# Order of the routing stage around the last output projection in a FoX and differential attention layer with a mixture of experts

## The chip, the cores and the metric

The kernel runs on one core of one Trainium2 chip. The metric is the device time of one execution in microseconds (us). Engines are named as in the profile: PE is the matmul engine, PEld its weight load, DVE the vector engine, ACT the scalar engine, POOL the GpSimd engine, and SP the queue that issues the DMA transfers.

## The reference, cut to what matters

One layer handles 256 prompt rows and 8 x 16 sample rows of width 1024, 384 rows in all (three row tiles of 128). Attention ends in an output projection with a residual. Then comes the mixture of experts, which the change is about:

```python
h = h + o @ w_out                                   # (384, 1024)
hn = h * rsqrt(mean(h * h) + 1e-6) * ffn_norm
logits = hn @ w_router + b_router                   # 32 experts
top_val, top_idx = top_k(logits, 4); gates = softmax(top_val)
# for each expert e, over the rows that chose it:
hcat = hn[rows] @ w_gate_up[e] + b_gate_up[e]       # (., 2048)
glu, lin = min(hcat[:, 0::2], 7), clip(hcat[:, 1::2], -7, 7)
y[rows] += gate * ((glu * sigmoid(1.702 * glu) * (lin + 1)) @ w_down[e] + b_down[e])
```

All data is float32. The weights of the 32 experts are 32 x (8 MB + 4 MB) and are streamed from HBM once.

## The kernel before, in words

Every engine has its own program, in an order written out by hand; they meet at semaphores (`wait_ge` and `then_inc`). There is no planner. `link` makes an engine wait for its own last instruction.

**The projection.** `project_out(n)` is one column half of one row tile (tile n // 2, half n % 2): 8 products of 128x128 by 128x512, each recorded as two passes, so 16 rows of the trace (L1672). DVE adds each half to the residual rows y in `residual(n)` (L1233, semaphore y_added).

**Routing a row tile t.** PE turns the tile (`turn_rows`, 8 transposes, L1706), ACT and DVE move four turned blocks each to SBUF with the norm's gain (`hT_evac`, L897 and L1250), PE forms the 32 logits (`logits`, L1715, 16 passes). ACT sums the squares (`square`, L879), DVE makes the mean, ACT the root (`root`, L884), DVE the reciprocal (`invert`, L1256), ACT scales the rows to x2n (`scale`, L889). DVE's `route` (L1265 to L1273) finds the four best experts and the 0/1 table M of rows by experts, `gate` the softmax weights. PE's order is: halves 2, turn 0, half 3, logits 0, half 4, turn 1, half 5, logits 1, turn 2, logits 2.

**Ranks, selection, gather.** After that PE multiplies M by a strictly triangular table `before` and by ones (L1734 to L1740), which gives each row's rank within its expert. DVE forms the table RK from it (L1313 to L1317). POOL's `build_sel` compares two columns of RK (the two experts of a pair) with 0..63 and so makes a selection matrix `sel` of 384 x 128 slots (L662, six instructions), then one with the gates in it, `selg` (L672). `gather` on PE multiplies x2n by `sel` (24 products, 48 passes, L1750); ACT and DVE move the result to XT (L927, L1339).

**The pairs.** Sixteen pairs of experts follow (`run_pairs`). In each, PE adds the bias (L1759), runs the gate and up products (128 passes of 512 columns, L1769), gathers for the next pair, and runs the down products (64 passes, L1801) and the scatter (L1816). The weights come in 2 MB pieces, 12 for a pair and 192 in all, through a ring of 8 slots. The first 8 pieces are loaded ahead (the last two of them after half 5, since the slots hold the projection's weights until then); each of the other 184 is issued by SP (L533) when PE has freed a slot (piece_done). PE frees the first two slots after the first quarter of the first pair's gate and up products.

Of the kernel before, what the change touches and what calls it, by code (L numbers as in the profile page):

```python
# [89 lines left out]
def build(nc, io, out):  # L90
    ctx = ExitStack()
    with ctx:
# [105 lines left out]
        rt = at(a0 + 11264, 512)  # L198
        bgu4 = at(hn0, 512)
# [4 lines left out]
        pRK = [at3(hn0 + 2336 + 16 * i, 3, 2) for i in range(2)]  # L204
        pG = [at3(hn0 + 2336 + 16 * i + 8, 3, 2) for i in range(2)]
        pO = at(hn0 + 2368, 1)
        OVI = at(hn0 + 2370, 164).bitcast(I32)
        IDX = at(hn0 + 2536, 8).bitcast(U32)
        own_e = [at(hn0 + 2544 + 128 * i, P) for i in range(2)]
        before = at(hn0 + 2800, P)  # L210
# [47 lines left out]
        rank_done, table_done = sem("rank_done"), sem("table_done")  # L258
# [77 lines left out]
        copy_no = {j: n + 1 for n, j in enumerate(copies)}  # L336

# [63 lines left out]
        def _(sp):  # L401
# [97 lines left out]
            for b in range(2, BATCH_D + 2):  # L499
                if b < BATCH_D:  # L500
                    sp.wait_ge(kc_T, 4 * (b - 1))
                    load_cache(b, "k")
                if b >= 4:
                    sp.wait_ge(mixed, NP + 2 * (b - 4) + 2)
                    load_cache(b - 2, "v")
                    load_v3(b - 2)
                if b in (4, 5):
                    s = {4: 5, 5: 3}[b]
                    sp.dma_start(piece_slot(s), piece_src(0, s - LEAD)).then_inc(ring_in[s], 16)
            sp.wait_ge(scored, NA)  # L510
# [8 lines left out]
            sp.dma_start(before, io["before"][:, :]).then_inc(s_bef, 16)  # L519
# [48 lines left out]
        def _(g_):  # L568
# [77 lines left out]
            def build_sel(u, pair, at_, r=None):  # L646
# [12 lines left out]
                for t in range(3):  # L659
                    for x in range(2):  # L660
                        cols = slice(SLOTS * x, SLOTS * (x + 1))
                        last = nc.gpsimd.tensor_scalar(sel[u][:, t, cols], C["iota"], pRK[u][:, t, x:x + 1], None, ALU.is_equal)  # L662
                last.then_inc(sel_ready, 1)

                nc.gpsimd.tensor_copy(own_e[u].rearrange("p (x s) -> p x s", x=2),
                                      C["eye4"][:, bass.ds(pair * 2, 2)].unsqueeze(2).to_broadcast([P, 2, SLOTS]))
                g_.wait_ge(gates_ready, 1)
                lk(nc.gpsimd.tensor_copy(pG[u], GT[:, :, bass.ds(pair * 2, 2)]))
                for t in range(3):
                    for x in range(2):  # L670
                        cols = slice(SLOTS * x, SLOTS * (x + 1))
                        last = nc.gpsimd.tensor_scalar(selg[u][:, t, cols], C["iota"], pRK[u][:, t, x:x + 1],  # L672
                                                       pG[u][:, t, x:x + 1], ALU.is_equal, ALU.mult)
                last.then_inc(selg_ready, 1)

            g_.wait_ge(table_done, 1)
            for u in range(2):
                build_sel(u, u, lambda c, u=u: 2 * u + c)
# [15 lines left out]
        def _(ac):  # L694
# [182 lines left out]
            def square(t):  # L877
                ac.wait_ge(y_added, 2 * t + 2)
                link(nc.scalar.activation(junk2, y[:, t], ACT.Square, accum_out=stat[:, 20 + t:21 + t]))  # L879
                nc.scalar.activation(stat[:, 40:41], stat[:, 20:21], ACT.Copy).then_inc(h_sq, 1)  # L880
# [11 lines left out]
            def hT_evac(t):  # L892
                ac.wait_ge(h_T, t + 1)
                if t == 2:
                    ac.wait_ge(logit_done, 1)
                for k in range(4):
                    last = nc.scalar.activation(XTr[t][:, k], banks[0][:, P * k:P * (k + 1)], ACT.Copy,  # L897
                                                scale=gcol[:, 8 + k:9 + k])
# [8 lines left out]
            root(0)  # L907
# [37 lines left out]
            gathered(lambda k, c: c, 0)  # L945
            run_pairs(ac, lambda it, u, at_, nx: pair(at_, u, nx))
# [11 lines left out]
        def _(ve):  # L958
# [281 lines left out]
            def mean(t):  # L1240
                ve.wait_ge(h_sq, t + 1)
                nc.vector.tensor_scalar(stat[:, 20 + t:21 + t], stat[:, 20 + t:21 + t], 1.0 / D, EPS, ALU.mult, ALU.add
                                        ).then_inc(h_ms, 1)

            def hT_evac(t):
                ve.wait_ge(h_T, t + 1)
                if t == 2:
                    ve.wait_ge(logit_done, 1)
                for k in range(4):
                    last = nc.vector.tensor_scalar(XTr[t][:, 4 + k], banks[1][:, P * k:P * (k + 1)],  # L1250
                                                   gcol[:, 12 + k:13 + k], None, ALU.mult)
                last.then_inc(hT_v, 1)

            def invert(t):
                ve.wait_ge(h_rt, t + 1)
                nc.vector.reciprocal(stat[:, 24 + t:25 + t], stat[:, 24 + t:25 + t]).then_inc(h_rc, 1)  # L1256
                ve.wait_ge(h_rc, t + 1)

            def route(t):
# [3 lines left out]
                ix = rt[:, 16 * t + 8:16 * t + 16]  # L1263
                ve.wait_ge(logit_done, t + 1)
                link(nc.vector.scalar_tensor_tensor(out=L, in0=banks[(2, 6, 7)[t]][:, 0:32], scalar=stat[:, 24 + t:25 + t],  # L1265
# [5 lines left out]
                link(nc.vector.tensor_scalar(M[:, t], C["iota"][:, 0:E], ix[:, 0:1], None, ALU.is_equal))  # L1271
                for j in range(1, TOPK):
                    ins = nc.vector.scalar_tensor_tensor(out=M[:, t], in0=C["iota"][:, 0:E], scalar=ix[:, j:j + 1],  # L1273
                                                         in1=M[:, t], op0=ALU.is_equal, op1=ALU.add)
                    if j < TOPK - 1:
                        link(ins)
                ins.then_inc(route_done, 1)

            def gate(t):

                ix = rt[:, 16 * t + 8:16 * t + 16]
                g4 = rt[:, 64 + 16 * t:68 + 16 * t]
                tmp = [rt[:, 256 + 32 * j:288 + 32 * j] for j in range(3)]
# [3 lines left out]
                nc.vector.tensor_scalar(GT[:, t], C["iota"][:, 0:E], ix[:, 0:1], g4[:, 0:1], ALU.is_equal, ALU.mult)  # L1287
                for j in range(1, TOPK):
                    ins = nc.vector.tensor_scalar(tmp[j - 1], C["iota"][:, 0:E], ix[:, j:j + 1], g4[:, j:j + 1],
                                                  ALU.is_equal, ALU.mult)  # L1290
                link(ins)
                for j in range(1, TOPK):
                    link(nc.vector.tensor_tensor(GT[:, t], GT[:, t], tmp[j - 1], ALU.add))

            residual(2)
            mean(0)
            hT_evac(0)
            residual(3)
            invert(0)
            mean(1)  # L1300
            route(0)
            gate(0)
            residual(4)
            hT_evac(1)
            invert(1)
# [6 lines left out]
            ve.wait_ge(rank_done, 1)  # L1312
            nc.vector.scalar_tensor_tensor(out=RK[:, 0], in0=banks[2][:, 0:E], scalar=1.0, in1=M[:, 0],  # L1313
                                           op0=ALU.add, op1=ALU.mult)
# [85 lines left out]
        def _(pe):  # L1400
# [354 lines left out]
            def pair(at_, u, arrived, next_at=None):  # L1755
# [6 lines left out]
                for k in range(8):  # L1762
                    if k % 2 == 0:
                        s = [arrived(k + x) for x in range(2)]
# [109 lines left out]
```

## Time and profile before

| | us |
|---|---|
| median of three runs | 1288.69 |
| lowest and highest run | 1286.04, 1290.76 |
| the profiled execution, whole | 1290.47 |
| its span from first to last instruction | 1288.7 |

In the profiled execution the matmul engine is busy for 95% of the span, DVE for 28%, ACT for 15% and POOL for 12%. The mean granted clock of the matmul engine is 0.972 of full speed. The core reads 442 MB from HBM. The page cuts the span into 40 slices of some 32 us; the routing stage lies in the slices from 300 to 354 us, and everything after it is the sixteen pairs. A busy share of a whole span hides such stages, so the rows further down are of single stretches.

### The profile page before, as it was taken

Reading aid. Unit: us, or ns where it says so; the run is one execution under the profiler, and the core shown is the slowest. Engines: PE = TensorE matmul, PEld = TensorE weight load, DVE = VectorE, ACT = ScalarE, POOL = GpSimd, SP = SyncE. Lnnn points to the kernel's source line nnn. Section 1 sums busy time; section 2 is a strip of 40 time slices with the busy share of each in tenths; the row PEclk is TensorE's granted clock in tenths of the full one; section 3 lists DMA queues with packets and bytes.
Section 4 is the critical chain, followed back from the end, with each engine's and each line's share of the span. In section 5 each row is a group of like instructions: output and inputs, shape, how many; then the busy total and the mean of one; then the engine's idle time right before and its main releaser. Section 6 shows DMA issues by size and latency. Waiting matters only on the chain.

```text
span 1288.7 us, 16163 instructions
## 1 busy us (share of the span) xinstructions
PE 1229.9 (95%) x6079; PEld 545.4 (42%) x6080; DVE 354.7 (28%) x947; ACT 198.4 (15%) x523; POOL 158.3 (12%) x378
## 2 busy tenths in 40 slices
PE   7999989899899999999999999999999999999987
PEld 3444355554643434344343434343443434343422
DVE  2233355532422212142221212131321212131412
ACT  3211264322400101010010101010100101010100
POOL 0032302110302021020202022020202020120000
PEclk9999997989799999999999999999999999999998
DMA  8712521961379999999999999999999999999993
GB/s 266 272 53 105 213 82 66 356 215 83 145 324 427 427 429 428 428 430 427 429 429 426 430 429 427 430 429 427 429 430 427 429 429 427 429 429 427 427 429 146
DMA packets 55049, 447.53 MB, mean 347 GB/s; under 512 B 11089, under 2 KB 11490, under 8 KB 30434
## 3 DMA queue, kind: packets, MB, share of 16 engines
q1 hardware_dynamic: 54400, 446.87, 83.6%
q8 instruction: 24, 0.39, 0.1%
q10 hardware_dynamic: 610, 0.14, 0.0%
q14 instruction: 15, 0.12, 0.0%
HBM read 442.13 MB, written 4.86 MB: 347 GB/s over the span
## 4 chain that ended last, share of the span: by engine, by line
PE 67%; DMA 27%; DVE 3%; ACT 1%; issue 1%; POOL 1%; SPq 1%; ACTq 0%; POOLq 0%; DVEq 0%
DMA arena<-in_w_gate_up 24%; PE psum L1801 17%; PE psum L1769 17%; PE psum L1506 8%; PE psum L1750 7%; PE psum L1672 3%; PE psum L1816 2%; PE psum L1784 1%; PE psum L1780 1%; DMA arena<-in_w_in 1%; PE psum L1543 1%; DMA arena<-in_cache_diff_k 1%; PE psum L1640 1%; PE psum L1573 1%; PE psum L1561 1%
## 5 line engine op out<-in xcount | busy, mean ns | idle before, releaser
L1769 PE MATMUL psum<-arena 128*64 128x512 f32 x2048 | 450.6, 599 | 20.7 <-DMA arena<-in_w_gate_up 20.2
L1769 PEld LDWEIGHTS psum<-arena 128*64 128x64 f32 x2048 | 153.2, 138 | 316.2 <-issue 316.2
L1801 PE MATMUL psum<-arena 128*64 128x512 f32 x1024 | 224.6, 596 | 0.8
L1366 DVE TENSOR_SCALAR arena<-psum 128x256 f32<-128x256 f32 x64 | 26.7, 417 | 434.1 <-PE psum L1769 432.3
L1801 PEld LDWEIGHTS psum<-arena 128*64 128x64 f32 x1024 | 78.7, 138 | 135.9 <-issue 134.6
L1506 PE MATMUL psum<-arena 128*128 128x512 f32 x288 | 128.7, 601 | 5.0 <-DMA arena<-in_w_in 4.5
L934 ACT ACTIVATE arena<-arena 128x256 f32<-128x256 f32 x64 | 26.7, 417 | 632.6 <-DVE arena L1366 632.6
L1750 PEld LDWEIGHTS psum<-arena 128*128 128x128 f32 x768 | 89.8, 197 | 16.1 <-issue 16.1
L1750 PE MATMUL psum<-arena 128*128 128x128 f32 x768 | 92.8, 282 | 3.9 <-POOL arena L662 3.9
L655 POOL COPY arena<-arena 128x6 f32 (+1 forms) x16 | 3.0, 190 | 759.4 <-PE psum L1801 704.3
L1816 PE MATMUL psum<-arena 128*128 128x512 f32 x192 | 93.2, 622 | 0.0
L1506 PEld LDWEIGHTS psum<-arena 128*128 128x128 f32 x288 | 53.9, 192 | 70.3 <-issue 63.3
L1384 DVE TENSOR_TENSOR arena<-psum,arena 128x512 f32<-128x512 f32 x96 | 66.4, 692 | 25.3 <-PE psum L1816 25.3
L1379 DVE COPY arena<-psum 128x512 f32<-128x512 f32 x16 | 11.1, 692 | 219.6 <-PE psum L1801 219.6
L1816 PEld LDWEIGHTS psum<-arena 128*128 128x128 f32 x192 | 28.6, 188 | 64.3 <-DVE arena L1384 42.1
L672 POOL TENSOR_SCALAR arena<-arena 128x64 f32<-128x64 f32 x96 | 54.1, 586 | 0.0
L1672 PE MATMUL psum<-arena 128*128 128x512 f32 x96 | 42.4, 595 | 1.0 <-DVE arena L1233 1.0
L662 POOL TENSOR_SCALAR arena<-arena 128x64 f32<-128x64 f32 x96 | 40.4, 448 | 0.0
L1354 DVE TENSOR_TENSOR arena<-arena 128x256 f32<-128x256 f32 x64 | 36.4, 610 | 5.4
L942 ACT ACTIVATE arena<-psum 128x512 f32<-128x512 f32 x16 | 9.6, 599 | 162.0 <-PE psum L1801 162.0
L1368 DVE SCALAR_TENSOR_TENSOR arena<-arena 128x256 f32<-128x256 f32 x64 | 27.3, 426 | 2.2
L1672 PEld LDWEIGHTS psum<-arena 128*128 128x128 f32 x96 | 17.8, 190 | 22.1 <-issue 20.6
(239 smaller groups left out, 810.6 us busy)
## 6 DMA issues: line engine op xcount, KB each, us to landing
arena<-in_w_gate_up SPq DMA_DIRECT2D x128, 2048.0 KB, 25.1
arena<-in_w_down SPq DMA_DIRECT2D x64, 2048.0 KB, 23.0
arena<-in_w_in SPq DMA_DIRECT2D x5, 2048.0 KB, 14.6
arena<-in_cache_fox_k SPq DMA_DIRECT2D x8, 512.0 KB, 5.6
arena<-in_cache_diff_k SPq DMA_DIRECT2D x8, 512.0 KB, 6.4
arena<-in_cache_fox_v SPq DMA_DIRECT2D x8, 512.0 KB, 6.8
arena<-in_cache_diff_v SPq DMA_DIRECT2D x8, 512.0 KB, 8.1
arena<-in_w_out SPq DMA_DIRECT2D x4, 1024.0 KB, 7.1
```

The costliest lines, as they stand in the source:

```text
L662: last = nc.gpsimd.tensor_scalar(sel[u][:, t, cols], C["iota"], pRK[u][:, t, x:x + 1], None, ALU.is_equal)
L672: last = nc.gpsimd.tensor_scalar(selg[u][:, t, cols], C["iota"], pRK[u][:, t, x:x + 1], pG[u][:, t, x:x + 1], ALU.is_equal, ALU.mult)
L934: nc.scalar.activation(sg[n % 2], tg[n % 2], ACT.Sigmoid, scale=1.702).then_inc(sig_ready, 1)
L1354: nc.vector.tensor_tensor(act_rows[:, 32 * n:32 * (n + 1)], ta[n % 2].rearrange("s (p q) -> s p q", q=8), sg[n % 2].rearrange("s (p q) -> ...
L1368: lk(nc.vector.scalar_tensor_tensor(out=ta[n % 2], in0=tl[n % 2], scalar=1.0, in1=tg[n % 2], op0=ALU.add, op1=ALU.mult))
L1384: nc.vector.tensor_tensor(y[:, t, cols], banks[4 + n % 2], y[:, t, cols], ALU.add).then_inc(y_added, 1)
L1506: last = mm(z_bank(u), hnT[:, k, r0:r0 + n], wv[:, k], start=(k == 0), stop=(k == 7))
L1672: last = mm(banks[4 + n % 2], oT[:, k, P * t:P * (t + 1)], wv[:, k % 2, 512 * hf:512 * hf + 512], start=(k == 0), stop=(k == 7))
L1750: last = mm(banks[6 + k // 4][:, P * (k % 4):P * (k % 4 + 1)], x2n[:, t, P * k:P * (k + 1)], sel[u][:, t], start=(t == 0), stop=(t == 2))
L1769: last = mm(banks[n][half], XT[u][:, k, half], piece_slot(s[x])[:, c0:c0 + 512], start=False, stop=(k == 7), skip_group_check=True)
L1801: last = mm(banks[hf][half], actT[:, 4 * i + c, half], w, start=False, stop=(i == 1 and c == 3), skip_group_check=True)
L1816: mm(banks[4 + n % 2], gT[:, P * t:P * (t + 1)], rows[:, 512 * hf:512 * hf + 512], start=True, stop=True).then_inc(scat_done, 1)
```

## The change

- The last row tile is handled by column halves: `turn_rows`, `hT_evac`, `logits` and the squares take a part of the blocks each, so that the left half is done before the right half of the projection is. A turned block k now lies where `turned_row(k)` says.
- PE's order: the turn of tile 1 stands in the middle of half 4; half 5 holds the left turn of tile 2 (before its product 4) and the ranks of tiles 0 and 1 (before its product 6). Then the left logits, the right turn, the gather's products of tiles 0 and 1 with the right logits between them, the last tile's ranks, its gather, and the totals.
- DVE's table is made in two steps; POOL builds the selection of tiles 0 and 1 in `first_two`, DVE that of tile 2. The table keeps rank plus 1 and is compared with `places` = 1..64.
- `route` and `gate` compare all four choices in one instruction of 128 elements and add them up in one reduction (EQ, EG), in place of chains of 32-element instructions.
- POOL computes the norm's inverse root as a power of -0.5 (`inverse`), in place of DVE's mean, ACT's root and DVE's reciprocal.
- `gates(2)` and `gate(2)` come after the first gather has been moved to XT. In a pair PE waits for `own_ready` at the bias, for the ACT half of XT at product 0, for the DVE half at product 4, and for `selg` only at its turning.
- `before` is loaded ahead of the residual rows, not after half 5.

```diff
-            def root(t):
-                ac.wait_ge(h_ms, t + 1)
-                nc.scalar.activation(stat[:, 24 + t:25 + t], stat[:, 20 + t:21 + t], ACT.Sqrt).then_inc(h_rt, 1)
+            def inverse(t):
+                ms = stat[:, 20 + t:21 + t]
+                g_.wait_ge(h_sq, t + 1 + (t == 2))
+                if t == 2:
+                    nc.gpsimd.tensor_tensor(ms, ms, stat[:, 46:47], ALU.add).then_inc(h_ms, 1)
+                    g_.wait_ge(h_ms, 3)
+                nc.gpsimd.tensor_scalar(ms, ms, 1.0 / D, EPS, ALU.mult, ALU.add).then_inc(h_ms, 1)
+                g_.wait_ge(h_ms, t + 1 + (t == 2))
+                nc.gpsimd.tensor_tensor(stat[:, 24 + t:25 + t], ms, stat[:, 44:45], ALU.pow).then_inc(h_rc, 1)
+            def first_two():
+                pr = pRK[0][:, 0:2]
+                g_.wait_ge(first_table, 1)
+                nc.gpsimd.tensor_copy(pr, RK[:, 0:2, 0:2]).then_inc(p_first, 1)
+                g_.wait_ge(p_first, 1)
+                for t in range(2):
+                    for x in range(2):
+                        last = nc.gpsimd.tensor_scalar(sel[0][:, t, SLOTS * x:SLOTS * (x + 1)], places,
+                                                       pr[:, t, x:x + 1], None, ALU.is_equal)
+                last.then_inc(sel_ready, 1)
@@ POOL
+            inverse(0)
+            inverse(1)
+            g_.wait_ge(places_ready, 1)
+            first_two()
+            g_.wait_ge(bias_kept, 4)
+            own_rows(0, 0)
+            inverse(2)
             g_.wait_ge(table_done, 1)
@@ ACT
             square(0)
-            root(0)
             hT_evac(0)
             scale(0)
             square(1)
-            root(1)
+            hT_evac(1)
             gates(0)
-            hT_evac(1)
             scale(1)
-            square(2)
-            hT_evac(2)
-            root(2)
+            square_half(0)
+            hT_evac(2, (0, 1))
+            gates(1)
+            square_half(1)
+            hT_evac(2, (4, 5))
             scale(2)
-            gates(1)
-            gates(2)
@@ DVE, route
-                link(nc.vector.tensor_scalar(M[:, t], C["iota"][:, 0:E], ix[:, 0:1], None, ALU.is_equal))
-                for j in range(1, TOPK):
-                    ins = nc.vector.scalar_tensor_tensor(out=M[:, t], in0=C["iota"][:, 0:E], scalar=ix[:, j:j + 1],
-                                                         in1=M[:, t], op0=ALU.is_equal, op1=ALU.add)
+                link(nc.vector.tensor_tensor(EQ[t], C["iota"][:, 0:E].unsqueeze(2).to_broadcast([P, E, TOPK]),
+                                             ix[:, 0:TOPK].unsqueeze(1).to_broadcast([P, E, TOPK]), ALU.is_equal))
+                nc.vector.tensor_reduce(M[:, t], EQ[t], AX.X, ALU.add).then_inc(route_done, 1)
@@ DVE, order
+            route(1)
+            hT_evac(2, (2, 3))
+            gate(1)
+            ve.wait_ge(rank_done, 1)
+            table(0, banks[2][:, 4 * E:5 * E])
+            table(1, banks[2][:, 5 * E:6 * E]).then_inc(first_table, 1)
             residual(5)
-            hT_evac(2)
-            mean(2)
-            route(1)
-            invert(2)
+            hT_evac(2, (6, 7))
             route(2)
+            ve.wait_ge(rank_done, 2)
+            table(2, banks[2][:, 6 * E:7 * E]).then_inc(table_done, 1)
+            ve.wait_ge(table_done, 1)
+            ve.wait_ge(places_ready, 1)
+            for x in range(2):
+                last = nc.vector.tensor_scalar(sel[0][:, 2, SLOTS * x:SLOTS * (x + 1)], places, RK[:, 2, x:x + 1], None,
+                                               ALU.is_equal)
+            last.then_inc(last_sel, 1)
@@ PE, order
-            project_out(4)
-            turn_rows(1)
-            project_out(5)
+            project_out(4, {4: lambda: turn_rows(1)})
             logits(1)
-            turn_rows(2)
-            logits(2)
+            project_out(5, {4: lambda: turn_rows(2, (0, 1, 2, 3)), 6: ranks_of_two})
+            logits(2, (0, 1, 2, 3))
+            turn_rows(2, (4, 5, 6, 7))
+            gather_first(0, (0, 1, 2, 3))
+            logits(2, (4, 5, 6, 7))
+            gather_first(0, (4, 5, 6, 7))
+            gather_first(1, range(8))
+            ranks_of_last()
+            gather_first(2, range(8))
+            totals()
```

## Rows read from the trace of the kernel before

**Rows 1.** Busy time by stretch: PE, PEld, DVE, ACT, POOL, granted clock, DMA share, GB/s.

```profile
410.10:466.40 56.30, 56.30 (x281) 22.62 (x277) 13.31 (x28) 5.67 (x12) 6.79 (x17) 1.00 1.01 426
629.00:688.00 59.00, 56.93 (x277) 23.16 (x277) 13.71 (x29) 5.68 (x12) 7.02 (x18) 1.00 1.00 427
```

**Rows 2.** The chain that ended last, in the pairs: start, length, what.

```profile
353.61 27.69 PE psum L1769 x128
381.29 5.55 PE psum L1750 x48
...
409.06 1.07 PE psum L1759 x8
410.13 27.62 PE psum L1769 x128
...
629.67 28.79 DMA arena<-in_w_gate_up
...
688.27 28.96 DMA arena<-in_w_gate_up
```

**Rows 3.** SP's own timeline, 330 to 420 us: start, length, what was issued.

```profile
330.75 1.82 SPq L521 DMA_DIRECT2D arena<-in_b_gate_up  x4
332.61 0.89 SPq L523 DMA_DIRECT2D arena<-in_b_down  x2
333.54 0.90 SPq L525 DMA_DIRECT2D arena<-in_w_gate_up  x2
360.86 7.75 SPq L533 DMA_DIRECT2D arena<-in_w_down  x4
```

**Rows 4.** The chain that ended last, 315 to 354 us.

```profile
315.65 6.95 PE psum L1672 x16
...
330.34 1.71 PE psum L1715 x16
332.05 0.92 PE psum L1706 x8
...
352.12 1.14 DVE arena L1339 x4
```

**Rows 5.** Timeline of DVE in the routing of tile 1: start, length, instruction.

```profile
334.10 0.24 DVE L1265 SCALAR_TENSOR_TENSOR arena<-psum,arena 128x32 f32<-128x32 f32 x1
...
335.17 0.24 DVE L1271 TENSOR_SCALAR arena<-arena 128x32 f32<-128x32 f32 x1
335.44 0.83 DVE L1273 SCALAR_TENSOR_TENSOR arena<-arena 128x32 f32<-128x32 f32 x3
```

**Rows 6.** Groups by line and shape, whole span: busy, mean ns, idle before.

```profile
L662 POOL TENSOR_SCALAR arena<-arena 128x64 f32<-128x64 f32 x96 | 40.4, 448 | 0.0
L635 POOL TENSOR_TENSOR arena<-arena 128x1 f32<-128x1 f32 x16 | 8.9, 556 | 1.3
...
L1354 DVE TENSOR_TENSOR arena<-arena 128x256 f32<-128x256 f32 x64 | 36.4, 610 | 5.4
...
L1069 DVE TENSOR_REDUCE arena<-arena 128x8 f32<-128x512 f32 x12 | 8.2, 686 | 49.1 <-ACT arena L781 49.1
...
L1233 DVE TENSOR_TENSOR arena<-psum,arena 128x512 f32<-128x512 f32 x6 | 4.0, 688 | 18.5 <-PE psum L1672 18.5
...
L1293 DVE TENSOR_TENSOR arena<-arena 128x32 f32<-128x32 f32 x9 | 1.7, 192 | 0.3
```

**Rows 7.** Stretches of 1 us, PE alone: length, busy, clock, DMA share, GB/s.

```profile
335.00:336.00 1.00, 1.00 (x11) 0.96 0.29 115
...
349.00:350.00 1.00, 1.00 (x8) 0.71 0.00 0
```

**Rows 8.** Timeline of PE where it resumed after waits: idle before in brackets.

```profile
299.07 7.13 PE L1672 MATMUL psum<-arena 128*128 128x512 f32 x16 [0.97 <-DVE arena L1233]
...
334.22 2.04 PE L1715 MATMUL psum<-arena 128*128 128x32 f32 x16 [1.26 <-ACT arena L897]
...
343.53 8.48 PE L1750 MATMUL psum<-arena 128*128 128x128 f32 x48 [3.85 <-POOL arena L662]
```

More of the change, by code:

```diff
@@ L658, in build_sel @@
                     lk(nc.gpsimd.tensor_scalar(pRK[u], pRK[u], pO, None, ALU.subtract))
[L659 to L666, printed above, removed]
+                if not first:
+                    for t in range(3):
+                        for x in range(2):
+                            cols = slice(SLOTS * x, SLOTS * (x + 1))
+                            last = nc.gpsimd.tensor_scalar(sel[u][:, t, cols], places, pRK[u][:, t, x:x + 1], None,
+                                                           ALU.is_equal)
+                    last.then_inc(sel_ready, 1)
+                    own_rows(u, pair)
                 g_.wait_ge(gates_ready, 1)
@@ L1237, in _, with hT_evac @@
             residual(1)
[L1240 to L1246, printed above, removed]
+            def hT_evac(t, ks=(2, 3, 6, 7)):
+                ve.wait_ge(h_T, t + 1 + (ks[0] == 6))
                 if t == 2:
                     ve.wait_ge(logit_done, 1)
-                for k in range(4):
-                    last = nc.vector.tensor_scalar(XTr[t][:, 4 + k], banks[1][:, P * k:P * (k + 1)],
-                                                   gcol[:, 12 + k:13 + k], None, ALU.mult)
+                for k in ks:
+                    last = nc.vector.tensor_scalar(XTr[t][:, k], turned_row(k), gcol[:, 8 + k:9 + k], None, ALU.mult)
                 last.then_inc(hT_v, 1)
[L1254 to L1257, printed above, removed]
             def route(t):
@@ L1286, in gate @@
                 link(nc.vector.tensor_scalar(g4, g4, stat[:, 32 + t:33 + t], None, ALU.mult))
[L1287 to L1293, printed above, removed]
+                link(nc.vector.tensor_tensor(EG, EQ[t], g4.unsqueeze(1).to_broadcast([P, E, TOPK]), ALU.mult))
@@ L1295, in _, with table @@
+                link(nc.vector.tensor_reduce(GT[:, t], EG, AX.X, ALU.add))
+            def table(t, rank):
+                return nc.vector.scalar_tensor_tensor(out=RK[:, t], in0=rank, scalar=1.0, in1=M[:, t],
+                                                      op0=ALU.add, op1=ALU.mult)
             residual(2)
-            mean(0)
             hT_evac(0)
             residual(3)
-            invert(0)
-            mean(1)
             route(0)
+            hT_evac(1)
             gate(0)
@@ L1713, in logits @@
                 pe.wait_ge(s_wrt, 16)
-                for k in range(8):
-                    last = mm(banks[(2, 6, 7)[t]][:, 0:32], XTr[t][:, k], w_rt[:, k], start=(k == 0), stop=(k == 7))
-                last.then_inc(logit_done, 1)
+                for k in ks:
+                    last = mm(banks[(2, 6, 3)[t]][:, 0:32], XTr[t][:, k], w_rt[:, k], start=(k == 0), stop=(k == 7))
+                if k == 7:
+                    last.then_inc(logit_done, 1)
+            R = banks[2][:, 4 * E:7 * E]
@@ new lines, in totals, with gather_first @@
+            def totals():
+                for t in range(3):
+                    last = mm(banks[4][:, 0:E], C["ones"], M[:, t], start=(t == 0), stop=(t == 2))
+                last.then_inc(rank_done, 1)
+            def gather_first(t, ks):
+                pe.wait_ge(h_n, t + 1)
+                pe.wait_ge(last_sel if t == 2 else sel_ready, 1)
+                for k in ks:
+                    last = mm(banks[6 + k // 4][:, P * (k % 4):P * (k % 4 + 1)], x2n[:, t, P * k:P * (k + 1)], sel[0][:, t],
+                              start=(t == 0 and k % 4 == 0), stop=(t == 2), skip_group_check=True)
+                    if t == 2 and k % 4 == 3:
+                        last.then_inc(xg_done, 1)
```

127 lines of the change are left out of this document (67 added, 60 removed).

## The prediction

> **What bounds the kernel now.** I read the profile in four steps: the pairs first, since they are three quarters of the time, then what sets their start, then the stage that the change touches, then the clock.
>
> The stretches of the pairs [rows 1] show PE and DMA both near 100%, which doesn't say which of them leads. The chain of waits does [rows 2]. An early pair takes 410.13 - 353.61 = 56.52 us, all of it PE work. From 629.67 on the chain goes through a transfer of gate and up weights in every pair, and a pair takes 688.27 - 629.67 = 58.60 us. So PE's need is 56.5 and DMA's is 58.6 us for a pair. DMA is the slower one; PE only lives on the ring's stock for the first pairs, and DMA is already at 1.01 of its time in the second pair, at 426 GB/s [rows 1]. The end is therefore set by the first refill plus 184 pieces of 58.60 / 12 = 4.88 us, and a tail on PE behind the last piece that the change doesn't touch.
>
> When is the first refill? SP issued the last two preloaded pieces at 333.54 and the first refill at 360.86 [rows 3]; at 335 to 336 us DMA was busy only in part, and at 349 us it was at zero [rows 7]. It is idle until PE frees two slots, 360.86 - 353.61 = 7.25 us after the first pair's first product. What moves the start of the first pair at 353.61 thus moves the end by as much, one to one, as long as the two preloaded pieces aren't what limits DMA.
>
> The start of the pair in turn hangs on the stage from 315.65 (half 4 begins) to 353.61, which is 37.96 us. In it the chain runs over PE alone up to 332.05 + 0.92 [rows 4], and then over DVE, PE and POOL by turns: PE stood for 1.26 us before the last logits and for 3.85 us before the gather [rows 8], and the gather took 8.48 us against 5.55 us for the same 48 passes in the pair [rows 2, 8]. The granted clock explains that: it fell from 1.0 to 0.5 (2.4 to 1.2 GHz) at the end of the stretch at 335 us, after the wait of 1.26 us, and rose again during 349 us [rows 7].
>
> **The change part by part, as what PE still has to do from 315.65 to the first product.** All at full clock.
> - Halves 4 and 5: 2 x 6.95 = 13.90 [rows 4].
> - Turns of tiles 1 and 2, 16 transposes at 0.92 for 8: 1.84. Logits 1 and 2: 2 x 1.71 = 3.42 [rows 4]. Splitting them adds no passes.
> - Ranks: 3 + 2 products and 3 for the totals, 16 passes. Before, six products with the same task ran mostly at half clock; the nearest row at full clock is the logits with 16 passes of 32 columns, 1.71 [rows 4]. One of the eight has 64 columns. I take 1.71.
> - The gather, same 48 passes in another order: 5.55. Bias: 1.07 [rows 2].
> Sum 27.49 us. Now the waits, by walking through the engines.
>
> Half 4 with its turn ends at 315.65 + 6.95 + 0.92 = 323.5; logits 1 follow at once, since the turned blocks of tile 1 are moved (1.14 us, as the four instructions in [rows 4]) while half 4's last products run. They end at 325.2. Half 5 with half a turn (0.46) and 6 rank passes (0.64) ends at 325.2 + 6.95 + 1.10 = 333.3. That is 3.0 us later than before (330.34), and it is what residual 5, the bias loads and pieces 6 and 7 wait for.
>
> Is the work inside half 5 ready? A route takes 335.17 - 334.10 = 1.07 us up to L1271 and then 0.24 + 0.83 and links, 2.2 in all [rows 5]. The four 32-element instructions become a comparison and a sum of 128 elements. The trace has neither: a tensor operation costs 0.19 us at 32 elements and 0.61 at 256, a reduction 0.69 at 512 [rows 6]. Interpolated by size I take 0.3 for each, so 1.7 for a route; the bounds are 0.2 and 0.65 each, 1.5 to 2.4. Route 1 starts with logits 1 at 325.2 and ends at 326.9, before PE comes to the ranks at some 330.9. Behind it on DVE stand two moves (to 329.9) and gate 1 (about 1.1, its chain of seven 32-element instructions gone; to 331.5). DVE then waits for the ranks, with residual 5 queued behind that wait. Ranks end at 331.5, two tables of 0.2 end at 332.0, and residual 5 is wanted only at 333.3: no cost, 1.3 us to spare. POOL's copy and four comparisons of 0.45 [rows 6] give the selection at 332.0 + 0.3 + 1.8 = 334.1.
>
> PE after half 5: left logits 333.3 to 334.15; residual 5 (0.69 [rows 6]) ends at 334.0; right turn to 334.65; gather of tile 0, left, to 335.6, its selection just ready; right logits need two moves of 0.3 on each of DVE and ACT, ready 335.5: to 336.45. Then 12 products of gather, 2.8 us, to 339.2. Meanwhile route 2 runs from 336.45 to 338.2. It also needs the inverse root: squares of the right half (ACT, 334.0 to 334.9), an addition, a mean and a power of 0.56 [rows 6] on POOL, so 336.0. That is 0.45 us before it is wanted, and what ACT's root, the reciprocal and their table loads cost is off the path anyway, as it was before behind route 1. Scaling of tile 2 (2.1 us) is done at 338.1, before its gather.
>
> The last tile's ranks take 0.45 after 339.2. Then comes the one bare wait: table 0.25, two comparisons on DVE about 0.45 (the trace has 0.24 for 32 elements [rows 5]; 0.4 to 0.7), handovers 0.15, together 0.85. The last gather's eight products follow. ACT's and DVE's moves to XT (1.14, on the path before [rows 4]) now lie beside totals and bias (0.65 + 1.07) and product 4's wait: nothing, and if that cover were gone 1.14. `gates(2)`, `gate(2)` and the second table of gates have until the pair's end. I add 0.3 for the small handovers between the pieces.
>
> So 27.49 + 0.85 + 0.30 = 28.64 us in place of 37.96: **9.3 us** less. The first product comes at 344.3, the first refill at 351.5. Pieces 6 and 7 are issued 3.0 us later less nothing but the 0.33 us of `before`, so at 336.2; together they are 2 x 4.88 us and end near 347. DMA still stands idle from there to 351.5, so the preload doesn't limit. Loading `before` ahead of y puts 64 KB, far less than 1 us, into a stretch where half 0 doesn't need y yet. In the loop itself `places` for the iota and a third semaphore change no instruction's size, and PE's later waits can win nothing where DMA leads.
>
> The granted clock is what I am least sure of. The Trainium skill ("TensorE: Matmul & The Clock Gate", section "A second HAM failure mode: psum-queue depth-cycling") says that frequent short idles between groups of matmuls make the clock swing between half and full rate. That speaks against the new order, which changes the kind of work ten times in 11 us; the trace agrees as far as the fall at 335 us goes, and the sum above stands at full clock, while with the rule it would be the first rival's.
>
> There is one rule on ports too. The Trainium skill ("SBUF — State Buffer", section "SBUF: two separate sides") states that DVE with two SBUF inputs and GpSimd reading SBUF shut each other out. POOL's selection here runs beside gate 1's end at most; by the rule it would cost one comparison of 0.3 us, a sum of 9.0 in place of 9.3.
>
> **The rivals.**
> - **The clock falls in the new order too.** For it: 1.26 us of waiting and thin work brought it down before [rows 7, 8]. Against: 0.97 us of waiting before half 2 didn't, since that half then ran 16 passes in 7.13 us [rows 8], and my longest wait is 0.85. Price: the same gather lost 8.48 - 5.55 = 2.9 us at half clock. If it falls before the last gather it also takes in totals, bias and the start of the pair: at most twice that, 6. Then the gain is 6.4, at worst 3.4: 1282.3, at worst 1285.3.
> - **The handovers cost more.** The walk has PE meeting its inputs within 0.1 us at three places (selection, right logits, inverse root). If DVE's 128-element instructions are at their upper bound, gate 1 is 0.7 later and the selection with it; each of three places may cost 0.5 to 1. Gain 7.3: 1281.4.
> - **It doesn't matter.** If DMA weren't the limit, or the preload was, the gain would be swallowed. [Rows 1, 2] speak against it: there is no idle DMA in any pair after the refills begin. Result 1288.7.
> - **Slower: half clock from within half 5 on.** The turn and ranks inside half 5 break its dense run. If DVE's route 1 came late there, PE would stand in the middle of the projection and the clock would drop at 331. PE work from there to the first product is some 13 us at full clock, and the first quarter of the pair, 7.25, lies behind it: all at half clock would cost 20 us against 9.3 gained, so 1299. It decides from about 9.3 us of PE work at half clock on. Before, half clock lasted 13 us of which PE worked 9, so that far it doesn't reach; and route 1 has 4 us to spare.
>
> **How the numbers follow.** Full clock as summed: 0.50. Clock falls: 0.25. Handovers: 0.17. No effect: 0.05. Slower: 0.03. The profiled execution took 1290.47 us, 1.8 above its span and 1.8 above the median of 1288.69; the sum gives 1281.2 for it and for the median 1288.69 - 9.3 = **1279.4**. The three runs spread by 2.4 us to either side, and 0.3% (3.9 us) is what can be told from no change. Low end: DVE's new instructions at their lower bound and no extra handovers give 0.8 more, and 1.6 for the spread: 1277.0. High end: the clock's worst price, 1285.3. Faster by over 0.3% means below 1284.8: all of the first three cases but the clock's worst part, 0.88. Within 0.3%: 0.09. Slower: 0.03.
>
> **What would show it.** Right: the first L1769 of the changed kernel at 344 to 345, the first refill some 7 us after it, half 5's last pass near 333, a single PE wait of about 0.85 before the last gather, and a DMA-led chain from about pair 4 or 5 on with 58.6 us for a pair. If the clock fell, a stretch of 0.5 stands between 336 and 352. Wrong: a PE wait of over 1 us at the selection of tiles 0 and 1 or inside half 5; DMA with gaps after the first refill; or pairs longer than 58.6 us, which nothing here foretells.

## The result, and the profile after

The changed kernel takes 1275.17 us (median of 10 executions, 1272.21 to 1282.28), the kernel before 1288.63 us (median of 10, 1283.35 to 1295.47). The medians lie 13.5 us apart. The ratio of the two over all their executions is 0.9903, with a 95% interval from 0.9877 to 0.9929: faster by 12.5 us, between 9.1 and 15.9. The forecast was 1279.4, its range 1277.0 to 1285.3. The time lies below the range. The gain of 9.3 us that was summed lies just inside the measured interval, so the first question is whether the sum or the range was at fault.

The profiled execution took 1273.09 us, with a span of 1271.3. This is its chain of work that ended last, from half 4 to the seventh pair (start, length, what), the answer to [rows 2, 4]:

```profile
310.04 3.52 PE psum L1700 x8
313.55 0.87 PE psum L1734 x8
314.43 3.44 PE psum L1700 x8
317.86 1.70 PE psum L1742 x16
319.57 3.52 PE psum L1700 x8
...
327.63 0.81 PE psum L1742 x8
329.07 0.89 PE psum L1770 x8
329.96 0.91 PE psum L1742 x8
330.87 2.76 PE psum L1770 x24
334.83 2.02 PE psum L1770 x16
337.45 1.07 PE psum L1810 x8
338.52 27.62 PE psum L1821 x128
...
614.43 28.77 DMA arena<-in_w_gate_up
...
673.01 28.92 DMA arena<-in_w_gate_up
```

Between half 4 and the first gate and up product (L1821 here, L1769 before) the chain has only two pieces that aren't PE's, the table and the selection of tile 2 on DVE (L1317 and L1341, 0.20 and 0.44 us), and none of POOL. Half 4 begins at 310.04, the first product at 338.45 in the timeline: the stage takes 28.41 us, where before it took 353.61 - 315.65 = 37.96 [rows 2, 4]. The sum had said 28.64. In the pairs nothing has changed: 673.01 - 614.43 = 58.58 us for one, through DMA.

The timeline of the last tile (all engines, start, length, idle before in brackets):

```profile
331.86 0.17 DVE L1301 CAST arena<-arena 128x8 f32<-128x8 uint32 x1
332.07 0.29 DVE L1302 TENSOR_TENSOR arena<-arena 128x128 f32<-128x128 f32 x1
332.39 0.29 DVE L1304 TENSOR_REDUCE arena<-arena 128x32 f32<-128x128 f32 x1
...
334.03 0.19 DVE L1317 SCALAR_TENSOR_TENSOR arena<-psum,arena 128x32 f32<-128x32 f32 x1 [1.35 <-PE psum L1759]
334.26 0.43 DVE L1341 TENSOR_SCALAR arena<-arena 128x64 f32<-128x64 f32 x2
...
334.83 2.02 PE L1770 MATMUL psum<-arena 128*128 128x128 f32 x16 [0.84 <-DVE arena L1341]
```

The two new DVE instructions take 0.29 us each (estimate 0.3), and the one bare wait is 0.84 us (estimate 0.85). SP and the clock stretches answer to [rows 3, 7]:

```profile
330.35 0.90 SPq L533 DMA_DIRECT2D arena<-in_w_gate_up  x2
345.73 7.75 SPq L541 DMA_DIRECT2D arena<-in_w_down  x4
```

```profile
334.00:335.00 1.00, 0.17 (x1) 1.00 1.04 442
...
342.00:343.00 1.00, 1.00 (x8) 1.00 0.00 0
```

The granted clock stays at 1.00 through the wait, and DMA stands idle from 342 us to the first refill at 345.73: the preload didn't become the limit. The sharing of ports between DVE and POOL that the prediction weighed didn't arise at the selection of tiles 0 and 1: gate 1 ended at 325.58, before POOL's copy at 326.36, and POOL's four comparisons took 1.71 us (estimate 1.8).

So the stage gave 9.55 us in this pair of traces, but the profiled executions differ by 1290.47 - 1273.09 = 17.4 us. The rest lies outside the stage: half 4 begins 315.65 - 310.04 = 5.6 us earlier, and from the first refill to the end of the span it is 1271.3 - 345.73 = 925.6 us in place of 1288.7 - 360.86 = 927.8. The projection ahead of half 4, where the change does alter some instructions of the other engines, is not the place. Here is its first half, before and then after:

```profile
283.88 7.13 PE L1672 MATMUL psum<-arena 128*128 128x512 f32 x16
```

```profile
278.26 7.13 PE L1700 MATMUL psum<-arena 128*128 128x512 f32 x16
```

From there to half 4 it is 31.8 us in both (315.65 - 283.88 and 310.04 - 278.26), and so in the further traces of either kernel in experiments 1, 2, 9 and 10. The 5.6 us thus lie ahead of the projection. Two theories were tested:
- **Chance:** the clock in the attention and behind the last transfer differs from execution to execution, and the change gives what the stage gives.
- **Systematic:** the stage before costs more than its one trace shows, or the change shortens something ahead of or behind it.

### The profile page after: what moved, and what is told of

It is laid out like the page before. It is cut to its first block, busy times and chain, and to the rows that moved or that the text cites. A ratio compares the mean times of both kernels' runs of the same rounds, so it can differ in the third digit from the quotient of the medians.

```text
span 1271.3 us, 16137 instructions
## 1 busy us (share of the span) xinstructions
PE 1217.8 (96%) x6083; PEld 536.0 (42%) x6084; DVE 350.7 (28%) x922; ACT 192.1 (15%) x515; POOL 160.4 (13%) x385
## 4 chain that ended last, share of the span: by engine, by line
PE 67%; DMA 27%; DVE 2%; ACT 1%; issue 1%; SPq 1%; POOL 0%; ACTq 0%; POOLq 0%
DMA arena<-in_w_gate_up 25%; PE psum L1854 18%; PE psum L1821 17%; PE psum L1532 9%; PE psum L1801 7%; PE psum L1700 3%; PE psum L1869 2%; PE psum L1836 1%; PE psum L1832 1%; PE psum L1569 1%; DMA arena<-in_cache_diff_k 1%; DMA arena<-in_w_in 1%; PE psum L1599 1%; PE psum L1587 1%; PE psum L1666 1%
## 5 line engine op out<-in xcount | busy, mean ns | idle before, releaser
L1821 PE MATMUL psum<-arena 128*64 128x512 f32 x2048 | 448.8, 597 | 20.4 <-DMA arena<-in_w_gate_up 20.4
L1821 PEld LDWEIGHTS psum<-arena 128*64 128x64 f32 x2048 | 150.9, 138 | 316.4 <-issue 316.3
L1801 PEld LDWEIGHTS psum<-arena 128*128 128x128 f32 x720 | 81.5, 192 | 12.2 <-issue 12.2
L1801 PE MATMUL psum<-arena 128*128 128x128 f32 x720 | 84.4, 276 | 0.0
L1532 PEld LDWEIGHTS psum<-arena 128*128 128x128 f32 x288 | 54.5, 194 | 69.6 <-issue 64.7
L1869 PEld LDWEIGHTS psum<-arena 128*128 128x128 f32 x192 | 28.6, 188 | 64.3 <-DVE arena L1405 42.1
L706 POOL TENSOR_SCALAR arena<-arena 128x64 f32<-128x64 f32 x96 | 54.2, 583 | 0.0
L697 POOL TENSOR_SCALAR arena<-arena 128x64 f32<-128x64 f32 x90 | 37.6, 443 | 0.0
L1110 DVE TENSOR_REDUCE arena<-arena 128x8 f32<-128x512 f32 (+1 forms) x14 | 9.6, 685 | 61.6 <-ACT arena L823 61.6
```

What stands on the lines that cost most here:

```text
L697: last = nc.gpsimd.tensor_scalar(sel[u][:, t, cols], places, pRK[u][:, t, x:x + 1], None, ALU.is_equal)
L706: last = nc.gpsimd.tensor_scalar(selg[u][:, t, cols], places, pRK[u][:, t, x:x + 1], pG[u][:, t, x:x + 1], ALU.is_equal, ALU.mult)
L1532: last = mm(z_bank(u), hnT[:, k, r0:r0 + n], wv[:, k], start=(k == 0), stop=(k == 7))
L1801: last = mm(banks[6 + k // 4][:, P * (k % 4):P * (k % 4 + 1)], x2n[:, t, P * k:P * (k + 1)], sel[u][:, t], start=(t == 0), stop=(t == 2))
L1821: last = mm(banks[n][half], XT[u][:, k, half], piece_slot(s[x])[:, c0:c0 + 512], start=False, stop=(k == 7), skip_group_check=True)
L1869: mm(banks[4 + n % 2], gT[:, P * t:P * (t + 1)], rows[:, 512 * hf:512 * hf + 512], start=True, stop=True).then_inc(scat_done, 1)
```

## The experiments

Each kernel was timed beside the kernel before, with 6 to 12 executions, except for experiment 12 with a single one. "Mean" is over all timed executions of a kernel, leaving out one of 2.5 ms (experiment 4) and one of 4.4 ms (experiment 1). "The stage" runs from the start of half 4 to the first gate and up product. "Half clock time" is the time in which the granted clock was 0.5: 2 x (1 - mean granted clock) x time.

**1, 9: the kernel before, unchanged.**

> The kernel before, unchanged, run against itself. It measures how much of a difference of two kernels is chance, and gives a second trace of the stage. Theory A (the stage gives 9.5 us in every execution, and what the timed difference has beyond that lies in the clock of stretches that the change doesn't touch): ratio 1.000 within its interval, the stage from half 4 to the first gate and up product again about 38 us, and the start of half 4 at another place than 315.65 us, anywhere from 310 to 320. Theory B (the stage before loses more to half clock than the one trace shows, since its clock stretch may last into the first pair): the stage takes 39 us or more, with the same start of half 4.

> The kernel before, unchanged, once more, for its trace and for more executions. Theory chance: the start of half 4 lies between 308 and 320 us as in the traces of the changed kernel, the stage takes 36.8 to 38 us, and over all executions the difference of the two kernels settles between 9 and 10.5 us. Rival (the change also shortens what lies ahead of the stage or behind it, by 2 us or more): the half clock time ahead of half 4 is again over 30 us, where the traces of kernels with the new order have 17 to 44, mean 31, and the difference settles at 12 us or more.

Ratios 1.0002 (0.9978 to 1.0027) and 1.0002 (0.9971 to 1.0033). PE where it resumed before the last gather, and at the first pair, in the first and in the second:

```profile
344.69 7.38 PE L1750 MATMUL psum<-arena 128*128 128x128 f32 x48 [3.84 <-POOL arena L662]
...
353.67 8.80 PE L1769 MATMUL psum<-arena 128*64 128x512 f32 x40 [0.52 <-DVE arena L1339]
```

```profile
339.50 7.06 PE L1750 MATMUL psum<-arena 128*128 128x128 f32 x48 [3.86 <-POOL arena L662]
...
348.15 4.08 PE L1769 MATMUL psum<-arena 128*64 128x512 f32 x18 [0.52 <-DVE arena L1339]
```

Half 4 began at 316.83 and 311.61, so the stage took 36.84 and 36.54 us. The waits are those of [rows 8] to 0.02 us; what differs is the gather, 8.48, 7.38 and 7.06 us, since the half clock lasted shorter. The stage before thus costs 37.1 us on average of three, not more than its first trace showed but less. The part of the systematic theory that has a costlier stage falls.

**2, 10: the changed kernel, unchanged.**

> The changed kernel, unchanged, again. Theory A: the stage from half 4 to the first gate and up product takes 28.5 us, and the start of half 4 moves by some us from run to run with the clock in the attention stage; the timed gain over before comes nearer to 9.5 us than the 13.5 us of the medians first seen. Theory B: the timed gain stays at 12 to 14 us, because before loses more at the stage than its trace showed.

> The changed kernel, unchanged, once more. Theory chance: stage 28.4 us, start of half 4 between 308 and 320 us, mean of the executions near 1278. Rival: mean near 1276.

Ratios 0.9924 (0.9896 to 0.9953) and 0.9916 (0.9884 to 0.9948). The stage took 28.41 us both times, but half 4 began at 315.11 and 310.25. The clock between (stretches of PE: length, busy, clock, DMA share, GB/s), in the first repetition and then in the second:

```profile
160.00:240.00 80.00, 71.97 (x523) 0.81 0.29 102
240.00:300.00 60.00, 53.19 (x530) 1.00 0.81 295
```

```profile
160.00:240.00 80.00, 71.92 (x578) 0.89 0.35 129
240.00:300.00 60.00, 55.31 (x491) 0.97 0.74 267
```

The same program had a mean clock of 0.81 or 0.89 in the same 80 us of attention. The kernel before had 0.87, 0.74 and 0.87 there in its three traces. Over all traces the start of half 4 lies between 308.6 and 317.2 us, for either order of the stage.

**3: before, with its waits filled.**

```diff
             turn_rows(2)
+            filler(5)
             logits(2)
 ...
+            filler(16)
             pe.wait_ge(s_bgu, 64)
+def filler(n): for _ in range(n): mm(banks[4][:, 0:P], C["ones"], C["ones"], start=True, stop=True)
```

> The kernel before with 5 extra products of ones ahead of the last logits and 16 ahead of the first gather, which keep PE busy in its two long waits. Their results are written to a PSUM bank that nobody reads. If the half clock of the stage is what a good part of the gain came from: the clock stays at 1.0, the gather takes 5.6 instead of 8.5 us, and the kernel is 3 to 3.5 us faster than before (0.9975). If the clock falls anyway or the extra products lie in the way: no gain, or 1 us slower.

Mean 1285.5 us against 1287.7; ratio 0.9984 (0.9957 to 1.0012), which timing alone can tell neither from no change nor from the expected 0.9975. Its PE timeline:

```profile
340.14 0.41 PE L1744 MATMUL psum<-arena 128*128 128x32 f32 x2 [1.12 <-DVE arena L1273]
340.61 5.45 PE L1720 MATMUL psum<-arena 128*128 128x128 f32 x32
345.89 5.52 PE L1756 MATMUL psum<-arena 128*128 128x128 f32 x48
...
353.01 9.23 PE L1775 MATMUL psum<-arena 128*64 128x512 f32 x42 [0.52 <-DVE arena L1339]
```

The gather took 5.52 us, as it does in the pairs. But the clock fell once more, from 341 to 345 us, and the fill of 16 products took 5.45 us where the wait was 3.85. The stage took 35.84 us: 1.3 under the mean of before. The expected 3 to 3.5 us didn't come in the stage: the gather gained 2.1 us on the mean of the three traces of before (7.64), but the fill, cut too long for the clock at which it ran, took 1.6 us more than the wait. It shows that the clock's share of the gather is 1.5 to 3 us (7.06 to 8.48, less 5.52).

**4: changed, the gather no longer fills the wait for the last route.**

```diff
-            gather_first(0, (0, 1, 2, 3))
             logits(2, (4, 5, 6, 7))
-            gather_first(0, (4, 5, 6, 7))
-            gather_first(1, range(8))
             ranks_of_last()
+            gather_first(0, range(8))
+            gather_first(1, range(8))
```

> The changed kernel with the gather of tiles 0 and 1 moved behind the last tile's ranks, so that it no longer fills the wait for the last logits and route. Prediction by the walk through the engines: PE now waits some 2.5 us for the last route, while the gather of tiles 0 and 1 hides the table and the selection of tile 2: net 2 us slower than the changed kernel if the clock stays at 1.0, 4 to 5 us slower if the wait of 2.5 us brings it down as it did in the kernel before. A rival (the order doesn't matter since DMA has room): no difference from the changed kernel.

```profile
336.49 1.05 PE L1742 MATMUL psum<-arena 128*128 128x32 f32 x8 [0.75 <-ACT arena L940]
337.38 0.39 PE L1757 MATMUL psum<-arena 128*128 128x32 f32 x2
339.41 0.64 PE L1759 MATMUL psum<-arena 128*128 128x32 f32 x2 [1.64 <-DVE arena L1304]
339.86 7.90 PE L1770 MATMUL psum<-arena 128*128 128x128 f32 x48
```

```profile
337.00:338.00 1.00, 0.77 (x7) 0.92 0.62 158
338.00:339.00 1.00, 0.00 (x0) 0.50 1.17 281
```

Half 4 began at 316.71 and the first product came at 349.34: 32.63 us, 4.2 more than the changed kernel; mean 1281.8, ratio 0.9952 (0.9927 to 0.9976). PE waited 0.75 and 1.64 us, and the 48 passes took 7.90 us in place of 5.55. The clock fell to 0.5 within the stretch at 337 us, whose mean is 0.92, that is as the second wait began and not after it. Of the 4.2 us, 2.35 are the clock's in the gather and the other 1.9 are put down to the order by subtraction. The size expected (4 to 5 us with a fall) held; that it would be the long wait that brings the clock down did not.

**5: changed, first pair later by 40 products.**

```diff
             gather_first(2, range(8))
+            for _ in range(40):
+                mm(banks[5][:, 0:P], C["ones"], C["ones"], start=True, stop=True)
             totals()
```

> The changed kernel with 40 extra products of ones (80 passes, 9.3 us) ahead of the totals, so that the first pair starts later by what the change took from the stage. Their results are written to a PSUM bank that nobody reads. Theory DMA leads from the first refill on: first gate and up product, first refill and the end all move by 9.3 us, 1277.2 (mean of 19 executions of the changed kernel) becomes 1286.5, which is within 2 us of before. Rival (a part of the stage's gain is given back later anyway, by the ring's stock): the end moves by less than 7 us.

```profile
341.76 9.10 PE L1792 MATMUL psum<-arena 128*128 128x128 f32 x80
...
352.45 13.10 PE L1823 MATMUL psum<-arena 128*64 128x512 f32 x60
```

Half 4 began at 315.11 as in experiment 2's trace, the first product came 8.93 us later than there, and the span was 1287.1 against 1278.6: 8.5 us. Mean 1289.1, ratio 0.9995 (0.9976 to 1.0015); the expected 1286.5 was 2.6 lower, and without one execution of 1303.2 us the mean is 1287.8. All of the stage's gain is undone by moving the start of the pairs alone. The rival, an end that moves by less than 7 us, is out.

**6: changed, 7 more products in each pair.**

```diff
                 pe.wait_ge(act_ready, at_(4, 4))
+                for _ in range(7):
+                    mm(banks[4][:, 0:P], C["ones"], C["ones"], start=True, stop=True)
                 for c in range(8):
```

> The changed kernel with 7 extra products of ones (14 passes, 1.6 us) in each of the 16 pairs, ahead of the turning of the activations, written to a PSUM bank before its next use. Theory DMA leads: PE's need per pair rises from 56.4 to 58.0 us and stays under DMA's 58.6, so 15 pairs cost nothing and only the last one's 1.6 us are seen: 1278.8. Rival (PE leads, or both do in turn): 16 x 1.6 = 26 us more, 1303.

The chain of two early pairs, and who PE waited for in all the pairs (total, times, longest):

```profile
453.08 27.62 PE psum L1821 x128
...
511.15 27.62 PE psum L1821 x128
```

```profile
PE psum L1821 <- DMA arena<-in_w_gate_up: 2.7, 2, 2.1
```

A pair now needs 58.07 us of PE. PE takes until the fourteenth pair to use up the ring's stock, and waits for DMA twice. From first refill to the end it is 1274.1 - 344.32 = 929.8 us, against 926.5 in the other traces on average: 3.3 us. Of these the 14 passes of the last pair take 2.55 (1.6 at full clock), since the clock was at 0.5 there; the rest is no more than the other traces differ by (924.9 to 927.9). Mean 1277.7. The rival's 26 us are out: DMA sets the pace.

**7: changed, the root on DVE and ACT again.**

```diff
+            def root(t):   # ACT; mean(t) and invert(t) on DVE, inverse(t) on POOL taken out
+                ac.wait_ge(h_ms, t + 1)
+                nc.scalar.activation(stat[:, 24 + t:25 + t], stat[:, 20 + t:21 + t], ACT.Sqrt).then_inc(h_rt, 1)
```

> The changed kernel with the norm's inverse root back on DVE (mean, reciprocal) and ACT (root), in place of the power on POOL. ACT's table loads of 1.28 us come back. Prediction: the last inverse root is ready some 0.4 us later than the last logits, the last route ends 0.4 us later, still ahead of the gather of tile 1 that hides it: 0 to 0.3 us, nothing that timing can tell. Rival (the power on POOL carries part of the gain): 1 us or more later at the first gate and up product.

```profile
336.17 1.28 ACT L947 ACT_TABLE_LOAD   x1
...
337.70 0.16 DVE L1333 RECIPROCAL arena<-arena 128x1 f32<-128x1 f32 x1 [1.31 <-ACT arena L947]
337.90 2.10 ACT L929 ACTIVATE arena<-arena 128x1024 f32<-128x1024 f32 x1 [0.23 <-DVE arena L1333]
337.90 0.25 DVE L1300 SCALAR_TENSOR_TENSOR arena<-psum,arena 128x32 f32<-128x32 f32 x1
```

DVE waits 1.31 us for the root, but route 2 begins only 0.5 us later within the stage, and the stage takes 344.86 - 316.46 = 28.40 us. Mean 1278.5, ratio 0.992 (0.9893 to 0.9947). The power on POOL carries none of the gain.

**8: changed, totals earlier and fill in the attention.**

```diff
+                if i in range(4, NP, 2):          # in turn_probs(i)
+                    pe.wait_ge(mix_copied, copy_no[i - 3])
+                    for _ in range(3):
+                        mm(banks[7][:, 384:512], C["ones"], C["ones"], start=True, stop=True, skip_group_check=True)
 ...
+            totals()
             gather_first(2, range(8))
-            totals()
```

> The changed kernel with two further edits. The totals stand ahead of the last gather and fill its bare wait of 0.84 us: first gate and up product 0.65 us earlier after the start of half 4. In the attention of the prompt rows PE gets 3 extra products of ones (0.7 us) ahead of every second turning of the probabilities from the fifth on, where it waits for ACT about 0.9 us each time and where the clock falls to 0.5 for 20 to 50 us in all the traces; their results are written to a PSUM part that nobody reads. If the waits bring the clock down: half clock time in the stretch from 170 to 230 us goes from about 30 to under 10 us, at 0.3 us of time for each us of half clock (the slope over 32 executions of before): 6 us faster than the changed kernel, 1271. If it is something else that brings it down (the next stage's waits, or chance): the same half clock time and 2 us slower.

```profile
160.00:240.00 80.00, 73.87 (x613) 0.94 0.35 128
240.00:300.00 60.00, 54.42 (x488) 0.97 0.72 266
```

The clock of the first stretch was 0.94, the highest seen, and half clock time from 60 us to half 4 was 14 us against 17 to 44. Yet half 4 began at 310.98, no earlier than in the best traces without fill (308.63, 310.04), and the mean of six executions is 1276.1, not the expected 1271. Half clock time is 33 us in these six and 46 in the changed kernel, yet they are only 0.8 us faster, of which the totals give 0.6. The fill seems to cost about what the clock gives; that is not shown, since no run separates the two.

**11: changed, totals earlier alone.**

> The changed kernel with the totals (6 passes, 0.65 us) ahead of the last gather instead of behind it, so that they fill a part of the bare wait of 0.84 us. First gate and up product 27.8 us after the start of half 4 instead of 28.4, and the mean 0.6 us lower, which the timing can't resolve. Rival (ACT's and DVE's moves to XT come onto the path, since the totals no longer cover them): 28.4 us or more.

```profile
336.00 0.83 PE L1763 MATMUL psum<-arena 128*128 128x32 f32 x6
337.00 2.02 PE L1770 MATMUL psum<-arena 128*128 128x128 f32 x16 [0.17 <-DVE arena L1341]
```

The wait shrank to 0.17 us and the stage to 340.02 - 312.20 = 27.82 us, 0.6 less, as in experiment 8. Mean 1278.3, ratio 0.9937 (0.9908 to 0.9966): by its trace the best version of the stage, by the timing not to be told from the changed kernel.

**12: changed, with the chains of 32-element instructions.**

> The changed kernel with the chains of 32-element instructions in route and gate again, in place of the comparisons and sums of 128 elements. A route is 0.5 us longer, a gate 1.0 us longer. Prediction: the last route still ends no later than the gather of tile 1 hides it; gate 1 is late by 1 us, and with it the first two tables and the selection of tiles 0 and 1: the gather of tile 0 waits 0.1 to 0.4 us. First gate and up product 28.5 to 28.9 us after the start of half 4. Rival (these chains were on the path): 1.5 us or more, 29.9.

```profile
335.52 1.13 PE L1781 MATMUL psum<-arena 128*128 128x128 f32 x8
...
341.63 2.02 PE L1781 MATMUL psum<-arena 128*128 128x128 f32 x16 [1.04 <-DVE arena L1352]
```

The stage took 345.24 - 316.40 = 28.84 us, 0.4 more. Half of it is in the last wait (1.04 for 0.84); the other half is ahead of the gather of tile 0, which starts 0.75 us after the right turn began, at 334.77, and in the changed kernel 0.50 (328.91 - 328.41). The fused comparisons are worth 0.4 us in the stage by this one trace; the single execution took 1282.19 us.

## Why the prediction missed

**What bounds the kernel: right.** A start of the pairs moved by 8.93 us moved the end by 8.5, and 1.6 us of PE work in each pair cost 3.3 in all. From the first refill to the end of the span all the traces but experiment 6's lie between 924.9 and 927.9 us, with either order of the stage.

**The sum: right.** Its terms, as predicted and as measured in the first trace: half 5 ends 17.65 and 17.59 us after half 4 began, a route takes 1.7 and 1.68, the bare wait is 0.85 and 0.84, the first product comes after 28.64 and 28.41, the first refill 7.25 and 7.28 behind it. The places called free were free: the root (experiment 7), the moves to XT (experiment 11). The stage gives 37.1 - 28.4 = 8.7 us on average over three traces of before and 9.55 against the one that was at hand, since that one had the longest half clock.

**The clock: the full-clock case held.** In the nine traces that keep the new order of the gather the stage ran at 1.00 throughout. The rule on frequent short idles, from the Trainium skill's "TensorE: Matmul & The Clock Gate", section "A second HAM failure mode: psum-queue depth-cycling", would have had it swing, and in these nine traces it didn't. The prediction's reason, that its longest wait of 0.85 us lay under one of 0.97 that had done no harm, isn't borne out, though: the length of the last wait doesn't sort the cases. Waits of 0.84 and 1.04 us in thin work passed without a fall. The clock fell after a wait of 1.26 us (before), after one of 1.12 (experiment 3) and after one of only 0.75 (experiment 4). What keeps the clock up in the new order is open.

**The step that failed is the low end of the range**: "no extra handovers give 0.8 more, and 1.6 for the spread: 1277.0". The term for the spread, 1.6 us, was read from three runs; its "2.4 us to either side" is half of the 4.7 between the lowest and the highest, and the farthest lay 2.7 from the median. Over 115 executions of before the standard deviation is 3.8 us, and they reach from 1280.3 to 1298.8. The spread goes with the clock: over the 105 with a record, time rises by 0.31 us for each us of half clock time, with a correlation of 0.92. In the traces half 4 begins at 308.6 us where 17 us of half clock lie between 60 us and it, and at 316.8 where 44 do. That the clock is the cause, and not longer waits that bring the clock down as well, is argued and not shown; experiment 8 cut the half clock time and gained almost nothing. The range let the clock take, on its high end, but not give on its low end, though the slice of the attention in the page of before showed it below full speed. With such a spread medians of ten executions move by 1 to 2 us: the changed kernel's were 1275.2, of nine 1279.0 and, of six, 1277.2. So the first median lay low in part by luck: the mean over all the executions counted below, 1278.2, lies inside the range and 1.2 us from the forecast.

**How much is the change worth?** 25 executions of the changed kernel have a mean of 1276.9 us, 115 of before 1287.7: 10.8 us, give or take 1.6. Experiments 4, 5, 7 and 11 have the changed kernel's program ahead of the stage and behind it. Less what their traces show in the stage (4.2, 8.9, 0, and -0.6 us), their means of 1281.8, 1289.1, 1278.5 and 1278.3 become 1277.6, 1280.2, 1278.5 and 1278.9. All 72 executions together give 1278.2, that is 9.5 us under before, give or take 1.2 (without the uncertainty of the four subtractions, each from one trace). That agrees with the stage's 8.7 to 9.55 and leaves at most some 2 us for an effect outside it. Half clock time is 45.7 us in the changed kernel and 67.0 in before, of which 10 to 14 us lie in the stage. In the 24 executions of experiments 7 and 11, also at full clock in the stage, it is 52 us, which leaves 1 to 5 beyond the stage instead of 7 to 11. Together with the overlap of the traces ahead of half 4 (17 to 44 us in the new order, 20 to 44 in the old) this speaks for chance, but doesn't show it. Of the stage's own gain 1.5 to 3 us come from the gather at full clock (experiment 3).

## What to carry to other kernels

Where a transfer stream leads the main loop, as here, the time is the start of the stream plus a nearly constant rest (925 to 928 us in thirteen traces); work out what the stage ahead of it costs by walking its waits, and don't look for gains in the loop. Order the work so that a matmul engine's wait for a short serial chain is filled with products that are needed anyway; filling 0.84 us of wait with 0.65 us of totals shortened the stage by 0.6 in two traces, and filling with useless products at an unknown clock gained less than expected both times. Before giving a range, look for stretches below full clock in parts that the change doesn't touch: they vary between executions, and here the spread went with them; and two profiles should be compared stage by stage and not by their spans.

## What was not expected of the hardware

The granted clock is not a property of the program: the same 80 us of attention ran at a mean of 0.74 and of 0.87 in two executions of the kernel before; what decides it is open. A microsecond at half clock went with only 0.31 us of time on average, presumably since part of it falls where PE isn't what the rest waits for; in the gather, where PE leads, 48 passes took 7.06 to 8.48 us instead of 5.55.
